# Two-layer block with a mixture of experts, one core: four modulation tiles between the router's products, and the first token half's products within the projection

## The reference, cut to what matters

```python
logits = xt @ router                              # 256 x 8
top_logit, top_e = lax.top_k(logits, 2)
gate = softmax(top_logit)
# tokens sorted by expert, each expert:
swiglu(xb, wg[e], wu[e], wd[e])                   # 1024 -> 3584 -> 1024
# second block, before its layers:
mod = cond @ w_ada[i] + b_ada[i]                  # 1024 -> 6144, two layers
```

## Time and profile before

| | |
|---|---|
| median of 3 runs | 2702.03 us (2700.46 to 2702.58) |
| the profiled execution | 2701.68 us |
| its span | 2699.9 us |
| TensorE busy in it | 2615.4 us, 97% |
| VectorE busy | 1183.8 us, 44% |
| mean granted clock | 0.991 |
| read from HBM | 626.82 MB |

### The profile page before, as it was taken

How to read it: one execution, slowest core, us unless ns; L and a number is a source line. 1 busy time by engine, 2 the same in 40 slices (tenths; PEclk the granted TensorE clock), 3 DMA queues, 4 the chain that set the end, 5 groups by cost and what they waited for, 6 DMA issues and landing times.

```text
span 2699.9 us, 48422 instructions
## 1 busy us (share of the span) xinstructions
PE 2615.4 (97%) x20513; PEld 1660.6 (62%) x20513; DVE 1183.8 (44%) x2860; ACT 446.8 (17%) x1058; POOL 108.7 (4%) x142
## 2 busy tenths in 40 slices
PE   7899999989999999999999999999989999999998
PEld 6659984865433333333333387699459957876993
DVE  5846675664111010110110166467655665344675
ACT  2331100233011011010110213300041001032000
POOL 1000000000100000000000011000010000040001
PEclk9999999999999999999999999999999999999999
DMA  7646555866999999999999946245405554231542
GB/s 220 217 156 214 164 170 178 280 242 252 300 420 419 420 411 418 412 410 419 412 419 411 401 147 109 71 157 172 171 17 173 171 172 133 70 94 63 183 165 90
DMA packets 237952, 642.99 MB, mean 238 GB/s; under 512 B 19769, under 2 KB 153281, under 8 KB 206896
## 3 DMA queue, kind: packets, MB, share of 16 engines
q1 hardware_dynamic: 230320, 618.02, 61.6%
q0 software_dynamic: 6752, 20.51, 3.4%
q10 hardware_dynamic: 672, 1.41, 0.1%
HBM read 626.82 MB, written 13.08 MB: 237 GB/s over the span
## 4 chain that ended last, share of the span: by engine, by line
PE 90%; DVE 8%; issue 1%; DMA 0%; POOL 0%; DVEq 0%; ACT 0%; ACTq 0%; POOLq 0%
PE pacc L1256 14%; PE pacc L1330 11%; PE pt L986 9%; PE pt L1330 7%; PE pacc L1347 7%; PE pt L1256 6%; PE pacc L1294 6%; PE po L1330 4%; PE pada L1356 4%; PE pt L1294 3%; PE pacc L1195 3%; PE pt L1233 2%; PE pt L1751 2%; PE pacc L1038 2%; DVE prob L2263 2%; PE pacc L1140 2%
## 5 line engine op out<-in xcount | busy, mean ns | idle before, releaser
L2604 DVE TENSOR_TENSOR gateb<-kT,pt 128x512 f32<-128x512 f32 (+1 forms) x32 | 19.9, 621 | 521.3 <-PE pt L1330 520.6
L986 PE MATMUL pt<-ring,hT 128*128 128x256 f32 x832 | 184.3, 381 | 3.0 <-DMA ring<-in_w_in 1.5
L1347 PE MATMUL pacc<-ring,bigc 128*32 128x512 f32 x1536 | 182.4, 592 | 0.0
L986 PEld LDWEIGHTS pt<-ring,hT 128*128 128x128 f32 x832 | 157.0, 190 | 28.4 <-issue 6.2
L1256 PE MATMUL pacc<-probT,prob 128*128 128x128 f32 x1440 | 170.6, 275 | 0.0
L1256 PEld LDWEIGHTS pacc<-probT,prob 128*128 128x128 f32 x1440 | 165.6, 192 | 0.0
L1330 PE MATMUL pacc<-ring,bigc 128*32 128x384 f32 (+1 forms) x1536 | 147.3, 539 | 0.0
L1294 PE MATMUL pacc<-prob,chunks 128*128 128x512 f32 x282 | 136.4, 592 | 0.0
L1330 PE MATMUL pt<-ring,bigc 128*32 128x384 f32 (+1 forms) x1280 | 131.6, 529 | 0.0
L2390 DVE TENSOR_TENSOR prob<-ring 128x512 f32<-128x512 f32 x86 | 59.5, 692 | 153.7 <-PE pacc L1256 107.0
L1347 PEld LDWEIGHTS pacc<-ring,bigc 128*32 128x32 f32 x1536 | 50.1, 110 | 114.7 <-issue 113.8
(11 more groups left out here) (471 smaller groups left out, 4259.2 us busy)
## 6 DMA issues: line engine op xcount, KB each, us to landing
ring<-in_moe_w_down SPq DMA_DIRECT2D x96, 1024.0 KB, 11.5
ring<-in_w_gate_up SPq DMA_DIRECT2D x66, 1024.0 KB, 5.1
ring<-in_w_ada SPq DMA_DIRECT2D x48, 1024.0 KB, 5.5
ring<-in_moe_w_up SPq DMA_DIRECT2D x48, 768.0 KB, 12.6
ring<-in_w_down SPq DMA_DIRECT2D x33, 1024.0 KB, 4.9
ring<-in_moe_w_gate SPq DMA_DIRECT2D x32, 1024.0 KB, 18.5
ring<-in_moe_w_up SPq DMA_DIRECT2D x32, 1024.0 KB, 19.0
ring<-in_moe_w_gate SPq DMA_DIRECT2D x32, 768.0 KB, 17.5
```

Source lines behind the costliest of these rows:

```text
L986: ins = pe.matmul(t[:, q * 256:q * 256 + n], src[:, k, q * P:q * P + P], w[:, k, 0:n], start=(k == 0), stop=(k == KC - 1))
L1347: ins = pe.matmul(down_main[32 * j:32 * j + 32, :], actT[:, 2 * t + k, 32 * g:32 * g + 32], w[:, k, 512 * h:512 * h + 512], start=(t == k ...
```

## The change

`MODS_ROUTER` goes from 2 to 4, and two of the 16 modulation tiles beside layer 1's attention go away: batches 0 and 9 have one tile in place of two. The order of all modulation tiles stays the same, so each of the others is done one or two places later. The list `stream` follows: behind the four tiles of the projection stand four modulation tiles and then the experts'. The router's products of the first token half move into the projection, behind its tile 2 of the second column half. The four last products of the second token half get a modulation tile in front of them, two follow behind, and one behind the counts. On VectorE two clears and the reciprocal for the first token half move ahead of its wait for the projection's last sum.

```diff
-MODS_BESIDE = ((1,) * 12, (2, 1, 1) * 4)
-MODS_ROUTER = 2
+MODS_BESIDE = ((1,) * 12, (1, 1, 1, 2, 1, 1, 2, 1, 1, 1, 1, 1))
+MODS_ROUTER = 4
...
-            def project_routed():
+            def project_routed(route_rows):
...
                         if h and t == 1:
                             turn_raw(1, range(4))
+                        if h and t == 2:
+                            route_rows(0, range(KC))
...
-                    project_routed()
                     t, filled, uses, emptied = bank()
-                    pe.wait_ge(emptied, uses)
-                    for q, blocks in ((0, range(KC)), (1, range(4)), (1, range(4, KC))):
-                        if q and blocks[0]:
-                            turn_raw(1, blocks)
+
+                    def route_rows(q, blocks):
+                        if q == 0:
+                            pe.wait_ge(emptied, uses)
                         pe.wait_ge(hT_ready, due("hT_ready"))
                         for k in blocks:
                             ins = pe.matmul(t[:, q * NE:q * NE + NE], hTv[:, k, q * P:q * P + P],
                                             router[:, k * NE:k * NE + NE], start=(k == 0), stop=(k == KC - 1))
-                    ins.then_inc(filled, 1)
+                        return ins
+
+                    project_routed(route_rows)
+                    route_rows(1, range(4))
+                    turn_raw(1, range(4, KC))
                     ada_tiles(1)
+                    route_rows(1, range(4, KC)).then_inc(filled, 1)
+                    ada_tiles(MODS_ROUTER - 2)
...
-                    ada_tiles(MODS_ROUTER - 1)
+                    ada_tiles(1)
                     turn_mod(48 // (KC // 2) - 1).then_inc(ada_done, 1)
...
                     ve.sem_inc(hT_ready, 1)
+                    ve.wait_ge(root_out, due("root_out"))
+                    go(ve.memset(yside, 0.0))
+                    go(ve.memset(stage, 0.0))
+                    link(ve.reciprocal(den[:, 2:3], den[:, 2:3]))
                     ve.wait_ge(sum_done, due("sum_done"))
...
-                    for q in range(QT):
-                        ve.wait_ge(root_out, due("root_out"))
-                        link(ve.reciprocal(den[:, 2 + q:3 + q], den[:, 2 + q:3 + q]))
-                    go(ve.memset(yside, 0.0))
-                    link(ve.memset(stage, 0.0))
+                    ve.wait_ge(root_out, due("root_out"))
+                    link(ve.reciprocal(den[:, 3:4], den[:, 3:4]))
```

## The result

The changed kernel takes 2705.36 us (median of 16 runs, 2702.89 to 2713.53), the kernel before, measured beside it, 2701.72 us (16 runs, 2700.19 to 2707.78). The ratio is 1.0017, with a 95% interval of 1.001 to 1.0024: 3.6 us slower, and by the interval 2.7 to 6.5. The profiled execution of the changed kernel took 2703.39 us around a span of 2701.6 us.

The account below looks back on a forecast made before the run. The order and landings of SyncE's transfers decide: tile 14 lands at 665.2 + 40.0 + 17.6 + 5.6 = 728.4 against 724.87, so the experts run 3.4 us later: 2702.03 + 3.4 = 2705.4, range 2702 to 2709.5.

Parts of the forecast that it names:

- Attention, 1.8 us earlier at the projection: Layer 1's attention: one tile less beside batch 0 and two turns off the chain, 0.93 + 0.54 + 0.35; bounds 0.9 and 2.8.
- SyncE's order: SyncE's queue: third modulation tile issued at 659.5, expert tiles only after; 17 tiles must land up to tile 14, not 11.
- Scatter 5.6 and gathers 17.6: Token transfers beside the expert stream: us each takes from the stream before tile 14 lands; scatter bounds 5.0 and 8.8.
- forecast landing of 728.4 for tile 14: Expert tile 14, counted from 0: 665.2 + 40.0 + 17.6 + 5.6 = 728.4 against 724.87, 3.5 us later.
- It isn't won back: Experts: the 3.4 us delay stays, since TensorE computes at 2.58 us a tile, slower than the stream.
- The routing: Projection to experts: experts start at 680.7 at full clock, 8.1 us earlier, or about 687 if the clock falls.
- The start counts, the stream doesn't: Rival at the experts' start: they start 8.1 us earlier and run through, 2693.9, or 2700 at low clock; chance 0.10.
- Its deciding point: Test of the early-start rival: it decides when more than 8 us of the stream's load vanish.
- The clock falls while TensorE is starved: Rival beside the gathers: TensorE drops to 1.2 GHz, 2.6 to 5.2 us on top, 2708.0 to 2710.6; chance 0.12.
- Small transfers cost more behind a full queue: Rival at the scatter: it costs 8.8 us, 3.2 more than taken, giving 2708.6; chance 0.16.

Follow-up runs that it names:

- e4: Changed kernel with three modulation tiles in the routing in place of four, and one more beside batch 9 of the attention: 2702.52 us, ratio 1.0003.
- e2: Kernel before with only the change's modulation tile lists (14 beside the attention, 4 in the routing): 2706.06 us, ratio 1.002.
- e7: Kernel before, with SyncE waiting for the release of the projection's first tile before issuing the first four expert tiles: 2702.69 us, ratio 1.0008.
- e1: Changed kernel with the first four expert tiles issued ahead of the routing's third modulation tile, as in the kernel before: 2701.00 us, ratio 0.9994.
- e5: Changed kernel with the gathers fetching only the rows of expert 1, one seventh of their bytes: 2697.81 us, ratio 0.9987.

## Why the prediction was right

The forecast was 2705.4 and the time 2705.36. The mechanism is the forecast one: the moved tiles hold back the experts' transfers, and the stream eats up the earlier start. That the numbers agree to 0.1 us is luck. The measured difference is known to 2.7 to 6.5 us only, the traces put the loss in the experts at 4.9 and not 3.4, and single terms were off by more.

- *Attention, 1.8 us earlier at the projection.* The projection starts at 636.71 against 637.68, 1.0 earlier. The attention of the changed kernel has 6.8 us at half clock, that of before 3.4, so its trace doesn't size the term; e4, with 3.4, has 69.8 us from the attention's start to the projection against 72.7, that is 2.9 less and above the bound of 2.8.
- *SyncE's order.* As forecast: third modulation tile at 660.2 (659.5 plus the 0.8 missing above), no expert tile before 662, share 0.00 and then 1. e2 shows the moved tiles to be the whole loss. By e7's trace the order alone costs 4.2 us, and e1 gets back 4.8 at tile 20.
- *Scatter 5.6 and gathers 17.6.* The scatter was mis-sized in kind. I counted its bytes in the stream, and not that a full queue makes it land 16.9 us after its issue instead of 4.9, and that the gathers wait for it. They start at 701.30 and not at 691.8, so only part of them falls ahead of tile 14, and TensorE waits at the tiles 15 to 18 and not at some of 10 to 14. The forecast landing of 728.4 for tile 14 is wrong: it was issued at 697.42 and landed 22.8 us later, at 720.2, just when TensorE came to it. Without gathers the sum would be 665.2 + 40.0 + 5.6 = 710.8, so 9.4 us of delay had reached tile 14, 0.7 of them from the later start. The rest came behind it: tile 18 landed at 738.8, 18.6 us later, where its four tiles need 2.5 + 3 x 1.87 = 8.1 alone. The sum for the experts came out at 4.9 in place of 3.4, of which 0.8 is the attention and 0.7 the transfers.
- *It isn't won back.* Right, and for the reason given, that TensorE is slower than the stream: from 1000 to 1100 it is busy for 100 us of 100, and both kernels take 757.8 us from expert 1 on. The stream gains on it, but only 0.8 us per expert.
- *The routing.* Experts start at 684.29, inside 680.7 to 687. The clock fell once, from 679.3 to 682.8, in the collecting, which took 5.41 where 3.4 was forecast for the full clock.

The rivals. *The start counts, the stream doesn't*: out, as 7 us of new waits show. Its deciding point, more than 8 us less load, was met in e5 (six sevenths of 17.6, 15.1 us less), and the sign flipped; but the time was 2697.8, not 2693.9, since the start was only 4.55 us earlier in the changed kernel, and in e5 2.0 us by the time from the projection on. *The clock falls while TensorE is starved*: it did, from 727.1 to 730.5, right behind the wait of 3.15 us for tile 15, as the Trainium skill describes it (TensorE: Matmul & The Clock Gate, HAM oscillation). Tile 15 took 4.7 us for the usual 2.6, but tile 16 landed only at 731.2, so it was covered. *Small transfers cost more behind a full queue*: not the scatter. From 690 to 700 it runs beside the stream in the changed kernel, and all engines together move 422 GB/s; what it costs there is its bytes, and the larger effect is its delay. The gathers are another matter. The queues in that stretch after, and in 700 to 720 before, beside the gathers (q1 is SyncE's, q0 GpSimd's: packets, MB, share of the 16 engines):

```profile
q1 hardware_dynamic: 398, 2.92, 69.4%
q0 software_dynamic: 358, 1.28, 31.5%
```

```profile
q1 hardware_dynamic: 482, 3.56, 69.4%
q0 software_dynamic: 485, 1.77, 31.4%
```

With the same shares of the engines the weights move 2.92 MB in 10 us beside the scatter and 3.56 MB in 20 us beside the gathers. So the gathers slow the weights' own packets too. (The prediction calls the scatter's rows as large as the stream's pieces; they are 4 KB and the stream's packets of a 1 MiB tile 8 KB.)

The Trainium skill (DMA: Bandwidth & Descriptors, Issuing engines are not separate DMA queues) says that the transfers of all issuing engines interleave on the same 16 engines. The trace agrees: both queues have a share in each of the two stretches. Bytes alone don't give the price: those of the gathers, 4 x 672 KB, are 6.6 us at 420 GB/s, and they took 17.6 from the stream.

## What to carry to other kernels

When a stage is shortened in front of a long stream of weights, work out first when the stream can deliver the tile at which its lead is used up; the earlier start is worth nothing until that tile comes earlier too. A piece of work that is moved takes its place in the load queue with it, and everything queued behind it moves too: check what fills the DMA engines in the gap that this leaves. A small dependent transfer pair (scatter, then gather) behind a queue that has just become full waits for it: here the gathers began 9.5 us later. Where loads and products of a long loop are nearly balanced (0.8 us won in an expert of 108 us here), such load can be hidden only as far as the slack reaches that is there already: to six gathers in the loop the experts lost 7.5 us, to three 1.8 to 2.1.

## What the runs showed of the hardware

- An indirect scatter of 128 rows of 4 KB landed 4.9 us after its issue with gaps in the stream, and 16.9 us behind a full queue. The DMA share alone doesn't tell it; what is issued ahead and hasn't landed has to be looked at: in the changed kernel the last tile ahead had 15.4 us to go, in e7, at a share of 1.01 too, 5.2 us, and there the scatter landed in 8.9.
- Four gathers of 672 KB pull the total of all engines down to 262 to 268 GB/s at a DMA share of 1.02. With 96 KB each, the stretch of 12 us that holds them moves 360. Beside a scatter of 4 KB rows the total stays at 422.
- Stretches at half clock fall at other places in other executions of the same instructions. TensorE's work is the same in the kernel before and in e7, and in their first 520 us it is at half clock for 13.7 us in the one trace and 20.5 in the other (granted clock 0.99 and 0.98). The changed kernel ran from 2702.9 (mean clock 0.992) to 2713.5, and its two slowest runs are those with a mean clock of 0.989; that spread is more than anything the change does.
